# Two weight pieces instead of one behind the last k-tiles of the output-projection slabs

## The reference, cut to what matters

```python
x = x + heads @ w_o                       # output projection, first ("o1") and second ("o3")
h = x * rsqrt(mean(x * x) + eps) * gain   # needs the whole of x, all 1024 columns
gate, up = split(conv(h @ w_up))          # next phase ("up1"); "up4" is its like after o3
x = x + (silu(gate) * up) @ w_down
```

## Time and profile before

| | before |
|---|---|
| median of 3 runs | 829.29 us |
| profiled execution, whole / span | 828.27 / 826.0 us |
| PE busy | 801.6 us (97%) |
| DVE busy | 644.4 us (78%) |
| ACT busy | 488.3 us (59%) |
| DMA | 179.44 MB, mean 217 GB/s |

### The profile page before, as it was taken

The page is one execution under the profiler, slowest core; times in us unless marked ns, Lnnn a source line. Parts: engine busy times, 40 slices in busy tenths (PEclk is TensorE's granted clock), DMA queues, the critical chain, the costliest instruction groups (busy, mean ns, idle before and its releaser), DMA issues. The chain is left out here.

```text
span 826.0 us, 16828 instructions
## 1 busy us (share of the span) xinstructions
PE 801.6 (97%) x6818; PEld 779.5 (94%) x6818; DVE 644.4 (78%) x1331; ACT 488.3 (59%) x1015; POOL 21.0 (3%) x53
## 2 busy tenths in 40 slices
PE   6999997999999999999999999899999999999998
PEld 5899997999999999999999999879889999999998
DVE  5788877988999886999888887777657897765651
ACT  6755556766666665755554646565655775555440
POOL 1000000000000000000000000700000000000000
PEclk9999999999999999999999999999999999999999
DMA  8776673766565987599998886625333677665540
GB/s 288 257 234 234 198 246 116 248 204 203 192 218 180 321 293 251 154 315 333 344 314 301 288 265 210 190 71 186 113 130 103 205 240 253 222 204 192 191 154 27
DMA packets 150013, 179.44 MB, mean 217 GB/s; under 512 B 5680, under 2 KB 139568, under 8 KB 149936
## 3 DMA queue, kind: packets, MB, share of 16 engines
q1 hardware_dynamic: 148624, 178.17, 65.7%
q0 software_dynamic: 1024, 0.03, 0.1%
q10 hardware_dynamic: 288, 0.16, 0.1%
HBM read 177.27 MB, written 1.05 MB: 216 GB/s over the span
## 5 line engine op out<-in xcount | busy, mean ns | idle before, releaser
L933 DVE TENSOR_TENSOR wlo<-raw,whi 128x512 fp32r<-128x512 f32 x528 | 343.3, 685 | 71.9 <-ACT whi L690 71.1
L1307 PE MATMUL bank<-A,whi 128*128 128x256 f32 x1280 | 364.1, 284 | 14.4 <-DVE wlo L933 7.5
L690 ACT ACTIVATE whi<-raw 128x512 fp32r<-128x512 f32 x528 | 308.3, 622 | 99.5 <-PE bank L1309 95.8
L1308 PE MATMUL bank<-A,whi 128*128 128x256 f32 x1280 | 356.9, 279 | 0.0
L1309 PE MATMUL bank<-A,wlo 128*128 128x256 f32 x1280 | 356.6, 279 | 0.0
L1307 PEld LDWEIGHTS bank<-A,whi 128*128 128x128 f32 x1280 | 243.1, 190 | 17.9 <-DVE wlo L933 9.0
L1308 PEld LDWEIGHTS bank<-A,whi 128*128 128x128 f32 x1280 | 243.2, 190 | 1.0 <-issue 1.0
L1309 PEld LDWEIGHTS bank<-A,wlo 128*128 128x128 f32 x1280 | 243.1, 190 | 0.0
L1307 PE MATMUL bank<-Hhi,whi 128*128 128x256 f32 x528 | 146.0, 276 | 0.0
L1309 PE MATMUL bank<-Hhi,wlo 128*128 128x256 f32 x528 | 145.7, 276 | 0.0
L1308 PE MATMUL bank<-Hlo,whi 128*128 128x256 f32 x528 | 145.7, 276 | 0.0
(11 more groups left out here) (148 smaller groups left out, 783.0 us busy)
## 6 DMA issues: line engine op xcount, KB each, us to landing
mring<-in_w_mod SPq DMA_DIRECT2D x72, 512.0 KB, 6.5
raw<-in_ffn_w_up SPq DMA_DIRECT2D x22, 1024.0 KB, 5.1
raw<-in_w_gate SPq DMA_DIRECT2D x22, 1024.0 KB, 5.7
raw<-in_w_up SPq DMA_DIRECT2D x22, 1024.0 KB, 5.8
raw<-in_w_down SPq DMA_DIRECT2D x16, 1024.0 KB, 5.8
raw<-in_w_in SPq DMA_DIRECT2D x12, 1024.0 KB, 5.7
raw<-in_moba_w_qkv SPq DMA_DIRECT2D x11, 1024.0 KB, 5.5
raw<-in_ffn_w_down SPq DMA_DIRECT2D x8, 1024.0 KB, 6.2
```

Source lines behind the costliest of these rows:

```text
L690: act.activation(whi[:, i % SPL, k0:k1, 0:width], raw[:, i % RAW, k0:k1, 0:width], ACT.Copy).then_inc(s_whi, 1)
L933: dve.tensor_tensor(lo, raw[:, i % RAW, k0:k1, 0:width], hi.bitcast(F32), ALU.subtract).then_inc(s_wlo, 1)
L1307: pe.matmul(o, hi, xh, start=kg == 0 and not (j and halved(g)), stop=False)
L1308: pe.matmul(o, hi, xl, start=False, stop=False)
```

## The change

In the five slabs of each output projection, behind k-tile 5, `fill` is called with 2 instead of 1. That is the last k-tile of the slabs with six and the sixth of the slab with eight.

```diff
@@ -349,7 +349,7 @@
                     self.chunk_done[i, kt // 2] = done
                     offer(i + SPL, kt + 1)
                     if i > 0:
-                        fill(1)
+                        fill(2 if tag in ("o", "ot") and kt == 5 else 1)
                     attend()
                 if i == 1 and kt == 5:
                     st.put("gq")
```

## The result

The kernel with the change takes 830.47 us (median of 20 runs, 829.35 to 832.80); the kernel before, timed beside it, 828.57 us (median of 20, 827.71 to 831.06). The ratio is 1.0022, interval 1.0013 to 1.0031: slower by 1.9 us where 2.05 us were forecast. The profiled execution, though, took 832.67 us whole, with a span of 830.5 us, 4.5 us more than before's 826.0. It is one of the slowest of its 20.

The account below looks back on a forecast made before the run. No engine's total changes, so the prediction looked at where TensorE stands still, at chains behind VectorE's queue. Terms: o1 +1.6, o3 and up4 together +0.45, sum +2.05 us on 829.29, giving 831.3 us; range 828.6 to 832.9.

Parts of the forecast that it names:

- (a): Slabs 12, 13, 14: one more copy and subtraction each before an attention step fits VectorE's idle time; cost 0.
- (b): Slab 15: extra subtraction between evictions of groups 0 and 1 waits for its copy behind ScalarE's squares; eviction 1.27 us later.
- (c): Slab 16: five subtractions instead of four before the last eviction, +0.62 us; that eviction about +1.9 us in all.
- (d): Slab 16: the 0.76 us wait for piece 16-3 goes but gives nothing; the gap before slab 17 only grows.
- (e): Slab 17: the clock gives back 0.3 of the 1.9 us; o1 term +1.6 us, ends +0.3 and +2.8.
- (g): o3: last eviction 1.25 us later, TensorE's 1.05 us wait becomes 2.3 us; bounds 0.6 and 1.9.
- (h): up4: three subtractions fewer before slab 108, so the 0.8 us wait for line 1132 goes: -0.8 us, bounds -0.8 and 0.
- (i): Loads go earlier; slab 16's first copy is used sooner without an earlier load: cost 0, at worst 0.5 us.
- B: Rival, faster: group 3's eviction begins when TensorE ends slab 16, up4's 0.8 us wait goes: -1.56 us, 827.7; chance 0.09.
- A: Rival: slab 17's slow clock stretch stays in time while the restart moves behind it; +0.75 us, 830.0; chance 0.18.
- C: Rival, worse: low clock covers the norm matmuls too and stays for slab 17; +3.2 us, 832.5; chance 0.17.
- D: Rival: nothing in effect, unseen idle time takes up the delays and waits gained are equal; 829.3; chance 0.10.

Follow-up runs that it names:

- e3: Changed kernel with the second piece only behind the last k-tile of the six-tile slabs, none in the transposed or eight-tile slabs: 827.31 us, ratio 0.9971 to the kernel before.
- e1: Changed kernel with the second piece only in the first output projection (slabs 12 to 16): 830.74 us, ratio 1.0015 to the kernel before.
- e8: Kernel before the change plus seven unread matmuls behind the second set of norm matmuls of up1: 828.08 us, ratio 0.9986 to the kernel before.
- e7: Changed kernel with two pieces behind the six-tile slabs' last k-tile, none behind the sixth and eighth k-tile of slabs 16 and 102: 827.20 us, ratio 0.9972 to before.
- e2: Changed kernel with the second piece only in the second output projection (slabs 100, 101 and 102 get one): 828.23 us, ratio 0.9984 to the kernel before.
- e9: e7 plus seven unread matmuls behind the second set of norm matmuls of up1: 826.06 us, ratio 0.9953 to the kernel before.
- e12: e9 plus four more unread matmuls in front of the fourth slab of qkv3: 824.23 us, ratio 0.9935 to the kernel before.
- e4: Changed kernel plus unread matmuls in up1, seven between the two sets of norm matmuls and nine behind the second: 827.47 us, ratio 0.9968 to the kernel before.
- e11: Changed kernel with the second piece only behind the fourth entry of the transposed slab, not the last: 828.36 us, ratio 0.9976 to the kernel before.

## Why the prediction was right, and where by luck

(a) Right: the extras in slabs 12, 13 and 14 cost nothing. VectorE's idle times of 0.99, 1.70 and 0.64 us became 0.38, 0.94 and none; of the third 0.04 us was left. e3 confirms it.

(b), (c) Right in place and size: +1.23 and +0.60 us, 1.83 in all where 1.9 stood.

(d) Right: the wait inside slab 16 went and gave nothing; the wait in front of the second norm set grew by 2.6 us.

(e) This step failed, although the sum came out right. I took 0.3 us as given back by the clock and set the ends of the o1 term at +0.3 and +2.8. The profiled execution had +3.55 and e1's +3.16, both beyond the end: the clock gave nothing back, it took 2.7 us more. What I had underrated is that the low level can cover the second norm set and more than half of slab 17 at once. What I had wrong is how before stood. I counted 1.6 us of low clock and waits there as if the clock could give them back; the 1.6 us were the low clock alone (16 matmuls 0.21 us apart instead of 0.11, no wait for A), but e8 shows that at full clock slab 17 would have waited 0.9 us for its own last piece. That piece comes early in the new order, so of the 1.83 us of delay only 0.93 is left when both kernels keep their clock.

**Where luck comes in.** The median is +1.9 us, o1 alone +3.55 and +3.16 us in the two profiles that have the whole delay and no added matmuls. Of the 20 runs 12 had a mean clock of 0.994 (median 829.97 us) and 8 a lower one (median 831.93 us). The two profiles at such clocks, e1's at 0.994 and after's at 0.992, both had about ten microseconds of low clock at slab 17; what sets them apart is the low clock in qkv3, which before's profile had and e1's hadn't. If they stand for the others, which isn't shown since only one of the 20 was profiled, most executions of the changed kernel lose over 3 us in o1 and save 1.6 us in qkv3 against before's profiled execution (828.27 us, near the median of 828.57), a stretch that the prediction doesn't look at. That would also answer why the profiled execution was so far off: it is one of those with both. The forecast's +1.6 for o1 is no stage's measured value.

(f) Nothing is to be seen for the five pieces fewer in up1, as predicted.

(g) The last eviction in o3 is 1.23 us later (11.94 against 10.71 us behind group 0's), where 1.25 stood. The wait for B rose to 1.7 instead of 2.3 us, because TensorE itself came to it 0.6 us later: slab 103 began 0.5 us later, behind a new wait of 0.34 us for group 2's later eviction (line 1166), which I had not listed. From group 0's eviction to the end of slab 103 the loss is 1.23 us, as counted; it is only spread over two waits.

(h) The wait for line 1132 went, and the stretch from slab 103 to slab 108 is 1.1 us shorter, against the 0.8 I counted. With (g) that makes +0.15 for +0.45.

(i) Right in the sum, loose in the detail. Copies did wait for loads:

```profile
ACT whi L690 <- DMA raw<-in_moba_w_o: 1.2, 1, 1.2
ACT whi L690 <- DMA raw<-in_ffn_w_up: 0.8, 1, 0.8
```

The first is the one I named, 0.7 us longer than my worst case; the second, slab 17's first copy, I hadn't seen. Both ended inside idle time.

Of the rivals, B's deciding point fell the way that the forecast had it, and e7 shows what it takes to turn it. A, the clock hiding the delay, is seen in no profile. C's mechanism is what the profiled execution and e1 show, the low clock over the second norm set and into slab 17, though the longer gap alone doesn't explain it; C's time, 832.5 us, is nearly the 832.67 of the profiled execution, and I gave it 0.17. D (nothing in effect) is excluded by the interval. That the low stretch differs from one execution to the next, on which A leaned, a single trace of before couldn't show; the table does: with the same gap of 5.8 us the clock was low for about 3 us in before and e2 and for about 7 in e7.

## What to carry to other kernels

Before more work is prefetched, look for the step that everybody waits for behind it in the same engine's list: a piece in front of it cost its full length each time here (0.6 us), and twice that where its input stood behind that step's partner on another engine (1.22 us); two places earlier it was free. Where a chain of small steps leaves TensorE idle, look at the granted clock behind it before pricing a delay: the same 1.83 us cost 0.93 us in o1 at full clock and 3.2 to 3.55 us with the clock as it fell. Matmuls that nobody reads, put into the gap, took 2.7 us of that back. And compare stages, not spans: one low stretch elsewhere that comes or stays away moves a span by 1.6 us.

## What the runs showed of the hardware that I had not expected

The low clock is no fixed tax on a gap. Before had two idle stretches of 0.4 and 3.2 us in a gap of 5.8 us and low clock for about 3 us; after had 3.0 and 3.25 us in a gap of 9.0 us (part of it the low clock's own doing) and low clock for about 10 us. In the table the low stretch is mostly the longer the longer the gap is, but e7 had 7 us with before's gap of 5.8 us, so the gap alone doesn't decide. From group 3's eviction slab 17 took 12.7 to 12.9 us to end with 3 us of low clock, 13.2 to 13.7 with 7, and 14.1 to 14.5 with 10. With seven unread matmuls of 128x256 behind the second norm set (e8, e9, e12), or seven ahead of it and nine behind (e4), the clock didn't fall there in any of the four profiled executions.

TensorE can lose time without any wait. In the changed kernel's profiled execution it started fewer matmuls between 150 and 200 us than before did, at full clock and with PE at 50.00 us busy in both:

```profile
150.00:200.00 50.00, 50.00 (x435) 50.00 (x435) 43.50 (x92) 34.26 (x73) 0.00 (x0) 1.00 0.58 190
```

```profile
150.00:200.00 50.00, 50.00 (x443) 50.00 (x443) 45.65 (x96) 34.09 (x73) 0.00 (x0) 1.00 0.63 206
```

The first is after, the second before. Between the first two line 1301 behind slab 17 the changed kernel took 28.49 us, before and the others 27.42 to 27.44. The matmuls start at one of two distances, 0.113 or 0.118 us, with a granted clock of 1.00 in both: after kept 0.118 from slab 17 to about 175 us, before changed to 0.113 at slab 17. e7 and e11 had 0.118 from about 240 to 325 us and lost 0.9 and 2.3 us in two such stretches of matmuls; e9 lost 1.8 us between 200 and 257 us. Around group 0's eviction in o1 the distance is 0.118 in all profiles but e9's, where it had fallen to 0.113; that is the quarter of a microsecond above. What sets it stays open.
